# Reciprocal roots with a three-step refinement in a decoder step, with the last norm regrouped

## What is computed

```python
def rmsnorm(x, g):
    xf = x.astype(jnp.float32)
    y = xf * lax.rsqrt(jnp.mean(xf * xf, axis=-1, keepdims=True) + EPS)
    return (y * g.astype(jnp.float32)).astype(x.dtype)
...
h = h + chunk_sgu(rmsnorm(h, norm_mix[0]), ...)      # layer 0; its v = rmsnorm(v, v_norm)
h = h + swiglu(rmsnorm(h, norm_ffn[0]), ...)
c, kr = shared_kv(h, ...)                            # latent c = rmsnorm(...), rotary key kr
h = h + attention(rmsnorm(h, norm_mix[1]), c, kr)    # layer 1; query side cq = rmsnorm(hn @ w_dq)
h = h + swiglu(rmsnorm(h, norm_ffn[1]), ...)
return rmsnorm(h, final_norm), c, kr, v
```

## Time and profile before

| what | us |
|---|---|
| median of 3 runs | 793.68 (793.11 to 794.12) |
| the profiled execution, its time | 794.5 |
| its span in the trace | 792.8 |
| PE busy | 756.6 (95%) |
| ACT, DVE, POOL busy | 402.9, 336.9, 548.2 |
| eight reciprocals on DVE (L802) | 12.8 |
| 12 table loads on ACT | 15.4 |

### The profile page before, as it was taken

How to read it: one execution, slowest core, us unless ns; L and a number is a source line. 1 busy time by engine, 2 the same in 40 slices (tenths; PEclk the granted TensorE clock), 3 DMA queues, 4 the chain that set the end, 5 groups by cost and what they waited for, 6 DMA issues and landing times.

```text
span 792.8 us, 17037 instructions
## 1 busy us (share of the span) xinstructions
PE 756.6 (95%) x6391; PEld 738.0 (93%) x6391; DVE 336.9 (42%) x779; ACT 402.9 (51%) x689; POOL 548.2 (69%) x255
## 2 busy tenths in 40 slices
PE   5899899999999999999999999999999999999994
PEld 5899899999999999999889777899999999999993
DVE  5897555424233232233876554543234233231114
ACT  6667444546444445555555464535555444444441
POOL 7676565987888878988777121216769887879880
PEclk9999899999999999999999999979999999999998
DMA  8454343655877655565475698613545655556641
GB/s 308 147 172 144 124 156 113 199 183 183 266 232 233 222 187 190 187 203 186 160 255 188 207 287 289 220 37 102 189 163 180 191 175 190 168 185 197 198 135 55
DMA packets 45495, 146.75 MB, mean 185 GB/s; under 512 B 5666, under 2 KB 6946, under 8 KB 45186
## 3 DMA queue, kind: packets, MB, share of 16 engines
q1 hardware_dynamic: 45298, 145.62, 56.2%
q0 software_dynamic: 144, 0.40, 0.1%
HBM read 144.52 MB, written 1.48 MB: 184 GB/s over the span
## 4 chain that ended last, share of the span: by engine, by line
PE 44%; DVE 3%; ACT 2%; issue 1%; ACTq 0%; DVEq 0%
PE ps L1238 14%; PE ps L1239 13%; PE ps L1240 13%; PE ps L1547 1%; ACT tt L703 1%; PE ps L1580 1%; PE ps L1523 1%; DVE work L802 0%; DVE h L1230 0%; DVE xlo L781 0%; PE ps L1469 0%; ACT xhi L709 0%; DVE tt L1125 0%; PE ps L1493 0%; PE ps L1593 0%
## 5 line engine op out<-in xcount | busy, mean ns | idle before, releaser
L392 POOL TENSOR_TENSOR wlo<-raw,whi 128x1024 fp32r<-128x1024 f32 x226 | 538.8, 2402 | 221.6 <-ACT whi L461 221.4
L1238 PE MATMUL ps<-xhi,whi 128*128 128x264 f32 x1076 | 312.0, 290 | 3.1 <-DVE olo L781 2.0
L1239 PE MATMUL ps<-xlo,whi 128*128 128x264 f32 x1076 | 307.6, 286 | 0.0
L1240 PE MATMUL ps<-xhi,wlo 128*128 128x264 f32 x1076 | 307.5, 286 | 0.0
L461 ACT ACTIVATE whi<-raw 128x1024 fp32r<-128x1024 f32 x226 | 237.9, 1054 | 53.0 <-PE ps L1240 50.2
L1238 PEld LDWEIGHTS ps<-xhi,whi 128*128 128x128 f32 x1076 | 205.7, 191 | 4.1 <-DVE olo L781 2.2
L1239 PEld LDWEIGHTS ps<-xlo,whi 128*128 128x128 f32 x1076 | 205.9, 191 | 0.2
L1240 PEld LDWEIGHTS ps<-xhi,wlo 128*128 128x128 f32 x1076 | 204.7, 190 | 0.0
L1238 PE MATMUL ps<-ahi,whi 128*128 128x264 f32 x352 | 100.0, 284 | 0.0
L1240 PE MATMUL ps<-ahi,wlo 128*128 128x264 f32 x352 | 99.9, 284 | 0.0
L1239 PE MATMUL ps<-alo,whi 128*128 128x264 f32 x352 | 99.9, 284 | 0.0
(11 more groups left out here) (244 smaller groups left out, 1158.8 us busy)
## 6 DMA issues: line engine op xcount, KB each, us to landing
raw<-w_stream SPq DMA_DIRECT2D x226, 512.0 KB, 3.4
pg<-pages SPq DMA_DIRECT2D x64, 288.0 KB, 3.6
pg<-w_ukT SPq DMA_DIRECT2D x1, 2048.0 KB, 8.1
pg<-w_uv SPq DMA_DIRECT2D x1, 2048.0 KB, 11.1
h<-xT SPq DMA_DIRECT2D x4, 264.0 KB, 4.5
y_out<-h SPq DMA_DIRECT2D x4, 264.0 KB, 2.1
raw<-w_stream SPq DMA_DIRECT2D x2, 256.0 KB, 3.2
wsraw<-wsT SPq DMA_DIRECT2D x1, 512.0 KB, 7.2
```

Source lines behind the costliest of these rows:

```text
L392: pool.tensor_tensor(wlo[:, c % RING, :], raw[:, c % RING, :], whi[:, c % RING, :].bitcast(F32), ALU.subtract).then_inc(lo_ready, 1)
L1238: pe.matmul(out, whi_, mhi, start=start, stop=False)
L1239: pe.matmul(out, whi_, mlo, start=False, stop=False)
L1240: return pe.matmul(out, wlo_, mhi, start=False, stop=stop)
```

## The change

It does five things.

- ACT takes `Abs_reciprocal_sqrt` in the place of `Sqrt`, so `yr` is already an inverse root.
- `refined` becomes three instructions with the same waits between them: `s = (s + K*EPS) * y`, `s = s * (-0.5/K) * y`, `R = (s + 1.5) * y`. The reciprocal is gone.
- `root` no longer loads the table. The table of the root is loaded ahead of the wait for the last residual chunk (`m == KD - 1`) in each `residual`, and at the start of the program. The norm v keeps its own load; q and lat need none, as before.
- The sum of the last norm is made in two products: ones times the sum of the first seven squares (`total`), and the eighth square, straight from ACT, added in PSUM. DVE's last addition is gone.
- The final gain is multiplied into `h` by ACT, tile by tile, each behind its square (`hg_done`). DVE's last step is four multiplications by `R`, two tiles (528 columns) each.

```diff
-STEPS = 4
+STEPS = 2
...
             def root(name, then=None):
                 q = NQ[name]
-                table(ACT.Sqrt)
                 act.wait_ge(sum_done, q + 1)
                 wait(act, rms_ready, q)
-                act.activation(yr[:], ps[:, 4, 0:T], ACT.Sqrt, bias=eps[:, 0:1],
+                act.activation(yr[:], ps[:, 4, 0:T], ACT.Abs_reciprocal_sqrt, bias=eps[:, 0:1],
                                scale=1.0 / NORMS[q][1]).then_inc(root_done, 1)
...
                 if name != "final":
                     gained(name, at)
+                else:
+                    act.wait_ge(sq_done, SQ0[NQ[name]] + m + 1)
+                    act.activation(h[:, at, :], h[:, at, :], ACT.Copy, scale=gn[:, G[name], at, :]).then_inc(hg_done, 1)
...
             act.wait_ge(const_done, 4)
-            table(ACT.Square)
+            table(ACT.Abs_reciprocal_sqrt)
...
             q = NQ["v"]
-            table(ACT.Sqrt)
+            table(ACT.Abs_reciprocal_sqrt)
...
                     for z in range(per):
                         split(s0 + per * m + AHEAD + z, i, per * k)
+                    if m == KD - 1:
+                        table(ACT.Abs_reciprocal_sqrt)
                     wait(act, psum_read, n0 + m + 1, i, k)
                     prepare(name, m, i, k)
...
             def add_square(q, m, i=0, k=0):
+                if q == NQ["final"] and m == KD - 1:
+                    return
...
-                last = isinstance(i, int) and m == NORMS[q][2] - 1
+                last = isinstance(i, int) and m == NORMS[q][2] - (2 if q == NQ["final"] else 1)
...
                 dve.wait_ge(root_done, q + 1)
-                dve.tensor_scalar(square, square, -0.5 / NORMS[q][1], -0.5 * EPS, ALU.mult, ALU.add).then_inc(norm_step, 1)
-                dve.reciprocal(y, y).then_inc(norm_step, 1)
+                n = NORMS[q][1]
+                dve.scalar_tensor_tensor(out=square, in0=square, scalar=n * EPS, in1=y, op0=ALU.add,
+                                         op1=ALU.mult).then_inc(norm_step, 1)
+                dve.wait_ge(norm_step, STEPS * q + 1)
+                dve.scalar_tensor_tensor(out=square, in0=square, scalar=-0.5 / n, in1=y, op0=ALU.mult,
+                                         op1=ALU.mult).then_inc(norm_step, 1)
                 dve.wait_ge(norm_step, STEPS * q + 2)
-                dve.tensor_tensor(square, square, y, ALU.mult).then_inc(norm_step, 1)
-                dve.wait_ge(norm_step, STEPS * q + 3)
-                dve.tensor_tensor(square, square, y, ALU.mult).then_inc(norm_step, 1)
-                dve.wait_ge(norm_step, STEPS * q + 4)
...
-            for m in range(KD):
-                dve.scalar_tensor_tensor(out=h[:, m, :], in0=h[:, m, :], scalar=gn[:, G["final"], m, :], in1=Ra[:],
-                                         op0=ALU.mult, op1=ALU.mult).then_inc(y_done, 1)
+            for m in range(0, KD, 2):
+                dve.wait_ge(hg_done, m + 2)
+                dve.tensor_tensor(h[:, m:m + 2, :], h[:, m:m + 2, :], Ra[:].unsqueeze(1).broadcast_to([P, 2, T]),
+                                  ALU.mult).then_inc(y_done, 2)
...
             ffn(1)
-            norm_sum("final")
+            q = NQ["final"]
+            pe.wait_ge(rms_ready, q)
+            pe.wait_ge(acc_done, ACC0[q] + KD - 1)
+            pe.matmul(ps[:, 4, 0:T], ones[:], total[:], start=True, stop=False)
+            pe.wait_ge(sq_done, SQ0[q] + KD)
+            pe.matmul(ps[:, 4, 0:T], ones[:], sq[:, (KD - 1) % 2, :], start=False, stop=True).then_inc(sum_done, 1)
```

More of the change, by code:

```diff
@@ L282, in build @@
                   "ohis_done", "olos_done"))
-        y_done = sem("y_done")
+        y_done, hg_done = map(sem, ("y_done", "hg_done"))
         XB = (6, 7, 4)
@@ L561, in _ @@
             q = NQ["v"]
-            table(ACT.Sqrt)
+            table(ACT.Abs_reciprocal_sqrt)
             act.wait_ge(sum_done, q + 1)
-            act.activation(yv[:], ps[:, 4, 0:NS + 2], ACT.Sqrt, bias=eps[:, 0:1], scale=1.0 / DS).then_inc(root_done, 1)
+            act.activation(yv[:], ps[:, 4, 0:NS + 2], ACT.Abs_reciprocal_sqrt, bias=eps[:, 0:1], scale=1.0 / DS).then_inc(root_done, 1)
             table(ACT.Gelu_apprx_tanh)
```

## The result

The changed kernel takes 782.58 us (median, 781.52 to 784.29, 4 runs), beside 793.9 (793.11 to 794.24, 4 runs) for the kernel before: the ratio is 0.9861, with a 95% interval of 0.9839 to 0.9883, that is 11.3 us less. The forecast was 781.1, in a range from 779.1 to 784.2. The profiled execution took 783.44, its span is 781.7.

A forecast was written before the change was run, and what follows sets the result against it. PE, busy 95% of the span, was taken as the bound, so gains come only at its stops, half clock and the end: 3.0 + 2.6 + 3.5 + 3.5 = 12.6 us less, 781.1 us, range 779.1 to 784.2.

The forecast's parts named there:

- q: At the norm q: PE's idle stretches of 0.67, 0.50 and 0.69 us go, with their filling; 2.6 us less.
- lat: At the norm lat: PE's stop before the next pair and the half clock behind it go; 3.5 us less.
- rival 2: Another half-clock stretch, behind v or at the attention's end, moves by one step of 3.4 us: 779.4 or 782.8; chance 0.2.
- mix0: At the norm mix0: PE's 2.19 us wait and the half clock behind it go, slab 4 gives some back; 3.0 us.
- v: Behind v: PE's wait for `wslo` does not hang on the refinement and stays, as does 6.8 us at half clock; 0.
- `cqlo` ... ends at 393.17 - 2.9 = 390.3: At q: `cqlo` ends 2.9 us sooner, before PE wants it at 391.1, so the 0.50 and 0.69 stops go.
- Rival 4: At q or lat: half is given back as ACT is late with `cqhi` or the next pair; 783.6; chance 0.1.
- ffn0, ffn1 and the tables: Refinement there is hidden under 8.5 us of PE work, and the moved table loads just fit ACT's idling; 0.
- Rival 3: On ACT: a table load costs a further 1.4 us, delaying squares ahead of inner norms; 782.4 to 785.2; chance 0.03.
- The end: Behind PE's last product: root 0.67 us sooner, refinement 2.16 less, results 0.75 less; taken as 3.5 us.
- Rival 1: At mix0 and lat: gaps close but the clock stays halved; 782.2 for one, 783.3 for both; chance 0.15.
- rival 5: In v's 16 chunks: DVE falls into step with POOL and becomes the bound, slower than before; chance 0.01.

The follow-up runs named there:

- end_only: Kernel before with only the new end (two-product sum, gain on ACT, two-tile results, table ahead of final's last residual); square root kept: 792.39 us, ratio 0.999.
- tables_only: Kernel before with only the square root's table loads moved ahead of the last residual chunk at ffn0, mix1, ffn1 and final: 793.95 us, ratio 1.0003.
- fix_v: Changed kernel with ScalarE's rounding of `wshi` moved ahead of the Gelu table load and a slab: 778.79 us, ratio 0.9801.
- late_q: Changed kernel with one extra, unused reciprocal, waited for, ahead of the refinement at q alone: 781.64 us.
- late_lat: Changed kernel with one extra, unused reciprocal, waited for, ahead of the refinement at lat alone: 783.16 us.
- fix_q: Changed kernel with ScalarE's three `cqhi` moved ahead of the slab that stood in front of them: 783.15 us, one run.
- fix_qk: fix_q with VectorE's two `krzlo` instructions moved back, one ahead of the sixth and one ahead of the seventh group of queries: 783.22 us, ratio 0.9852.
- late_hidden: Changed kernel with one extra, unused reciprocal, waited for, ahead of the refinements at ffn0 and ffn1: 783.08 us.
- refine_only: Kernel before with only the new root function and three-step refinement; table loads and end as they were: 784.15 us, ratio 0.9875.
- after_again: The changed kernel unaltered, measured once more against the kernel before: 782.27 us, ratio 0.9867.
- late_mix0: Changed kernel with one extra, unused reciprocal, waited for, ahead of the refinement at mix0 alone: 785.06 us, one run.

## Why the prediction was right, and where it was not

The total missed by 1.5 us and the signs were right. But the terms for q and lat were too large by 2.0 together, and part of that was made up by luck: in the traced pair 3.4 of the 6.8 us at half clock behind v went (1.53), which rival 2 had but the sum had not, and the start took 0.82 back.

- **mix0, 3.0 forecast, 3.03 between the two traces.** The wait is worth 2.17, from `end_only` to after (62.70 to 60.53). The slab's stop of 0.32 is there in `end_only` too, behind the long one, so at full clock it takes nothing back. At half clock, in before, it is absent, so it belongs to the price of the clock: 1.4 less 0.45 was forecast, 0.86 measured. The sizes were right; what was wrong is that every execution was taken to have the half clock. `end_only` and `tables_only` have the same stop without it, so for the median the term is 2.2 plus a share of 0.9.
- **v, 0 forecast.** The stop stayed at 2.56 for the reason given: `wslo` waits for `wshi`, and `fix_v` removes the stop by reordering ScalarE. What the forecast did not see is that the pair's 5.80 us are 2.48 when GpSimd is idle (`fix_v`). The half clock behind it was forecast to stay at 6.8. It was 3.4, which is rival 2 on its low side: 1.53 of the 11.05 between the two traces. It is no effect of the change, since `end_only` and `tables_only`, with the old refinement, have 3.4 as well.
- **q, 2.6 forecast, about 1.4 measured.** The sum's stop of 0.67 went with its filling (from mix1's sum to q's sum, 9.98 to 9.15, so 0.83), and from there to the stop at the rotary key it is 12.43 in the place of 13.04. The step that failed is "`cqlo` ... ends at 393.17 - 2.9 = 390.3". It took 4.57 us for a cost that moves along with its start. `cqlo` ends 0.69 behind GpSimd's series in both kernels, and the series moved by 1.47 only, with mix1's refinement, of which `gq` lost 0.7. The row told it: 4.57 for three instructions of 264 columns, when others of the kind take 0.43. `late_q` shows that q's own refinement is worth nothing; the 0.67 at its sum, too, is mix1's. The filling was put at 0.25 for each stop; it was 0.16 at this one and 0.29 at the stop of `late_lat` (1.82 less 1.53). Rival 4 had the size (2 to 3 us less for q and lat; it was 2.0) and the late `cqhi`, but that was not its cause, as `fix_q` shows.
- **lat, 3.5 forecast, 2.7 measured** (from the stop at the rotary key to the first product by `qns`: 39.37 before, 36.70 after). The stop of 1.96 and the half clock went. The question of the forecast, what is late next, was answered with 0.3 for the latent's copies on ScalarE; those cost PE nothing that shows, and `krzlo` on VectorE, two groups later, cost 0.70 and the filling, together 1.08, as `fix_qk` shows. That is the term that was mis-sized.
- **ffn0, ffn1 and the tables, 0 forecast, 0 measured**: `late_hidden`, `tables_only`. Rival 3 is out. Mix1 has no stop of its own either, and its part is counted at q, as in the forecast.
- **The end, 3.5 forecast, 3.23 measured** (column f), of which `refine_only` and `end_only` show 2.18 and 1.06. From PE's last weights to R there are 3.63 us, as forecast. The results took 2.56 for 2.6. The stores gave back 0.25 where 0.1 was allowed: from the last result to the end there are 2.48 us before and 2.73 after.
- **The start**, which no term covered, took 0.82 back in the profiled execution: mix0's sum at 19.08 for 18.26. No edit explains it, since the column varies as much among traces of like code (18.54 and 19.08 for the changed kernel).
- Rival 1 did not come true as put (no stop, no half clock, in all traces), rival 5 neither: b fell by all that mix0 had to give.

So 3.0 + 2.6 + 3.5 + 3.5 = 12.6 should have read about 2.2 to 3.0, 1.4, 2.7 and 3.2, that is 9.5 to 10.3. The two single parts, 9.4 and 1.2, add up to 10.6. The 11.3 of the whole lies 0.7 above, less than the 1.55 that 3.4 us more at half clock cost. The averaged clocks speak for such stretches: three of the four runs of `refine_only` have 0.987 or 0.988 (784.0 to 784.4) and one 0.989 (782.4), while of the eight runs of the changed kernel four have 0.990. Where the clocks are alike the two kernels lie about 1 us apart, as column f has it (10.34 to 9.29). For the medians this stays an argument.

## What to carry to other kernels

Cutting a chain pays only where the last wait of a stretch hangs on it. Before a long instruction is shifted in a forecast, ask whether its duration is its own: a duration several times that of its kind may end with some other engine's work, as `cqlo` does here, and then it will not move along. When a stop is removed, walk the next few groups on the engine that feeds the waiting one, and look there for instructions that share a port with a busy neighbour. And a stretch at half clock in one trace need not be a property of the code, as the ones at mix0 and behind v were not: price it by its share of executions, and compare kernels by stretches, cut at marks, before their times.

## What the runs showed of the hardware

- The same program, with the same order and, from mix0's sum to the attention, the same stops to 0.01 us (after and `after_again`), has stretches at 0.50 of different length: 3.4 or 0 behind v, and over all kernels here 0, 3.4 or 6.8 there and 6.8, 10.2 or 13.7 at the attention's end. 3.4 us more of it cost 1.55 us. A stop of 2.2 us at mix0 was followed by half clock in one trace of three, one of 1.96 at lat in all three that have it, one of 2.56 behind v in ten of twelve, and the stops of 1.85 in `late_mix0` and 1.53 in `late_lat` were not.
- VectorE's `cqlo` and the first `krzlo`, with two inputs in SBUF, end 0.28 to 0.29 us behind one of GpSimd's instructions when they run under its series: 2.61 us for 0.48. Starting `cqlo` 1.44 us earlier brought its end forward by 0.18. `wslo`, two of 128 x 1024, takes 5.80 us beside two subtractions and 2.48 with GpSimd idle.
- `Abs_reciprocal_sqrt` takes 0.48 us for 128 x 264, as the square root does at most norms (0.46 at the last, where the new one takes 0.48). The kernel has no load between it and the squares or copies around it.
- An activation starts 0.01 to 0.02 us behind the end of a table load of 1.28 us, at all 12 loads of the kernel before and all 11 of the changed one.
- A multiplication of 128 x 528 with an operand repeated over two tiles goes at four in 2.56 us, 0.64 each: no more per column than an ordinary one of 128 x 264 (0.43).
